# A convolution bias moved from the matmul engine to ScalarE, and segment sums with one stationary matrix and split rates moving

## The chip, the cores and the metric

One core of a Trainium2 chip runs the whole program. The time is the device time of that core in microseconds, from launch to end. Besides TensorE (PE), the engines are VectorE (DVE), ScalarE (ACT), GpSimd (POOL) and SyncE (SP), which issues most of the DMAs.

## The reference, cut to what matters

The program is one layer of a hybrid decoder for a prompt of 2048 tokens and 8 sample tokens. The change touches the Mamba-2 (SSD) mixer of the prompt. Its two pieces are a depthwise causal convolution with a bias, followed by silu, and a scan in chunks of 128 tokens, in which a lower triangle of sums of the rates `a` between two tokens is exponentiated:

```python
def causal_dwconv(xpad, w, bias):          # w: 4 taps, 896 channels
    y = bias
    for j in range(K):
        y = y + xpad[:, j:j + T] * w[j]
    return y

xbc_c = jax.nn.silu(causal_dwconv(xpad, conv_w, conv_b))
...
xr = jnp.where(jnp.tril(jnp.ones((T, T), bool), -1), a[..., :, None], 0.0)
ss = jnp.cumsum(xr, axis=-2)               # segsum: ss[l, s] = a[s+1] + ... + a[l]
scores = einsum(Cc, Bc) * jnp.exp(ss)      # per head, 6 heads, 16 chunks
```

All is in float32.

## The kernel before, in words

The program runs its stages one after the other: the input projection, forgetting attention (with the sample's paged cache beside it), `local_stage`, an output projection, and the channel mixer. Only `local_stage` is touched. It works on two things side by side. The first is dilated attention in 48 units of 128 queries (three dilation groups of 16 units). The second is the SSD mixer in 16 chunks of 128 tokens. A slot `s` holds one step of several units; a chunk takes three slots, called phase 0, 1 and 2 (`s % 3`). Each engine has its program written out slot by slot, in a fixed order, with semaphores between engines; no engine goes ahead of its own order.

What each engine does for a chunk `c`, in its order:

- PE, phase 0: the unit's `value`, `turn_p`, `score`, then `turn_x` of the chunk before (L1507; it waits for the activated x part and for `y_taken`, which DVE gives with L1411), `turn_in` (L1481, seven transposes of the raw input into the PSUM banks `conv_ps`), the unit's `turn` (L1446), and `segments` (L1530, six matmuls, one for each head, into two PSUM banks). Phase 1: `turn_b`, and `convolve(c, 0)` for one channel tile. Phase 2: `states`, `convolve(c, 1)` for three channel tiles, `outputs` (L1555). A channel tile is five matmuls: one with the bias on a diagonal against ones (L1496) and four with the taps on diagonals against shifted input (L1498).
- POOL: `xdd` (L1131) in phase 0, `mix` (L1140), `skip` (L1145) and the convolution of one x tile (L1112 to L1116) in phase 1, then in phase 2 `mask` of the next chunk (L1099): it multiplies a 128x128 step matrix by the rates of six heads, 768 elements a partition, into `a_mask`. These six products are the stationary sides of `segments`.
- ACT: among the units' copies and exponentials, `tanh` of the x part (L1255) and of the other four tiles straight from PSUM (L1259) in phase 2, `decay` = exp of the segment sums (L1240) in phase 0.
- DVE: the units' `copy_p` (L1308) and `maxima` (L1322 to L1328), the convolution of two x tiles (L1336, L1341) in phase 1, and in phase 2 the state (L1395, L1398), `y` from PSUM (L1400), then `activate(c, 0)` and `activate(c, 1)` (both L1355: (tanh + 1) times the convolved value; half 0 reads SBUF alone, half 1 reads its second operand from PSUM), then L1411 (y plus PSUM, gives `y_taken`), L1415, L1419.

The taps and the bias were halved beforehand, since silu is computed as x/2 (1 + tanh(x/2)). Before the loop the stage builds the diagonals (DVE L1281, ACT L1161), the gates and the distance biases of the attention.

Of the kernel before, what the change touches and what calls it, by code (L numbers as in the profile page):

```python
# [12 lines left out]
F32 = mybir.dt.float32  # L13
# [908 lines left out]
def local_stage(nc, inputs, pa, pb, toep_d, gates, ma, mc, p_ssm_d, p_conv_d, ahead_of_projection):  # L922
# [9 lines left out]
    with ExitStack() as ctx:  # L932
# [3 lines left out]
        def sem(name):  # L936
# [16 lines left out]

        a = sb("sp_a", [P, ALL_TILES, H])
        dt = sb("sp_dt", [P, ALL_TILES, H])
        e_cum = sb("sp_e_cum", [P, ALL_TILES, H])
# [3 lines left out]
        xT = sb("sp_xT", [P, 2, CT, C_CONV - 1 + P])  # L960
        diag = sb("sp_diag", [P, CT, C_CONV + 1, P])
        x_conv = sb("sp_x_conv", [P, XT, P])
        x_part = sb("sp_x_part", [P, P])
        tanh = sb("sp_tanh", [P, CT, P])
        sT = sb("sp_sT", [P, 2, CT, P])
        z2 = sb("sp_z2", [P, 2, C_INNER])
# [5 lines left out]
        b_tok = sb("sp_b_tok", [P, C_GROUPS, C_STATE])  # L972
        a_mask = sb("sp_a_mask", [P, H, P])
        decay = sb("sp_decay", [P, 2, H, P])
# [34 lines left out]
             "cb_ready", "mix_ready", "st_done", "off_ready", "y_done", "y_taken", "y_ready", "state_ready", "skip_ready",  # L1009
             "squared"))  # L1010
        fin_turned, fin_ready, out_done = sem("sp_fin_turned"), sem("sp_fin_ready"), sem("sp_out_done")
        dve, gps = Steps(sem("sp_dve")), Steps(sem("sp_gps"))
# [82 lines left out]
        def _(pool):  # L1095
            def mask(c):
                if c >= 1:
                    pool.wait_ge(seg_done, c)
                pool.tensor_tensor(a_mask[:], consts[:, TRI_GT].unsqueeze(1).to_broadcast([P, H, P]),  # L1099
                                   a[:, c + 1].unsqueeze(2).to_broadcast([P, H, P]), ALU.mult).then_inc(mask_ready, 1)  # L1100

# [19 lines left out]
            pool.wait_ge(inputs.landed, inputs.LANDED)  # L1121
            pool.wait_ge(gates_a, 1)
            mask(0)
# [31 lines left out]
        def _(act):  # L1155
# [3 lines left out]
            for k in range(5, CT):  # L1159
                for j in range(C_CONV + 1):  # L1160
                    last = act.activation(diag[:, k, j], ident, ACT.Copy, scale=taps[:, k, j:j + 1])  # L1161
            last.then_inc(diag_late, 1)
# [39 lines left out]
            for s in range(SLOTS):  # L1202
# [47 lines left out]
                if phase == 2 and now < TILES:  # L1250
                    act.wait_ge(x_conv_ready, now + 1)
                    act.wait_ge(x_conv_low, now + 1)
                    if now >= 1:
                        act.wait_ge(s_ready, 2 * now - 1)
                    act.activation(tanh[:, 0:XT], x_conv[:], ACT.Tanh).then_inc(tanh_ready, 1)  # L1255
                    act.wait_ge(conv_done, 2 * now + 2)
                    if now >= 1:
                        act.wait_ge(s_ready, 2 * now)
                    act.activation(tanh[:, XT:].rearrange("p c n -> p (c n)"), conv_ps[:, XT * P:CT * P], ACT.Tanh  # L1259
                                   ).then_inc(tanh_ready, 1)  # L1260

        @block.vector
        def _(v):
# [6 lines left out]
            v.tensor_tensor(a[:], dt[:], heads[:, 0].unsqueeze(1).to_broadcast([P, ALL_TILES, H]), ALU.mult  # L1270
                            ).then_inc(gates_a, 1)
            dve.link(v, v.tensor_scalar(taps[:], taps[:], 0.5, None, ALU.mult))
            v.sem_inc(taps_ready, 1)
# [5 lines left out]
            def diagonals(c, taps_of):  # L1279
                for j in taps_of:  # L1280
                    last = v.tensor_scalar(diag[:, c, j], ident, taps[:, c, j:j + 1], None, ALU.mult)  # L1281
                last.then_inc(diag_ready, 1)
# [14 lines left out]
            by_distance(4)  # L1297
            diagonals(XT, range(3, C_CONV + 1))
            by_distance(5)
            diagonals(XT + 1, range(C_CONV + 1))  # L1300
            v.wait_ge(gates_exp, 3)

# [46 lines left out]
            def activate(c, half):  # L1349
                lo, hi = (XT, CT) if half else (0, XT)  # L1350
                v.wait_ge(tanh_ready, 2 * c + half + 1)
                if c >= 2:
                    v.wait_ge(st_done, c - 1)
                pre = conv_ps[:, XT * P:CT * P].rearrange("p (c n) -> p c n", n=P) if half else x_conv[:]
                v.scalar_tensor_tensor(out=sT[:, c % 2, lo:hi], in0=tanh[:, lo:hi], scalar=1.0, in1=pre,  # L1355
                                       op0=ALU.add, op1=ALU.mult).then_inc(s_ready, 1)
# [69 lines left out]
        def _(pe):  # L1426
# [49 lines left out]
            def turn_in(c):  # L1476
                pe.wait_ge(landed[c % 2], 16 * (c // 2 + 1))
                if c >= 1:
                    pe.wait_ge(s_ready, 2 * c)
                for k in range(CT):  # L1480
# [4 lines left out]
            def convolve(c, half):  # L1485
# [8 lines left out]
                for k in range(*((4, CT) if half else (XT, 4))):  # L1494
                    at = conv_ps[:, k * P:(k + 1) * P]
                    pe.matmul(at, diag[:, k, C_CONV], consts[:, ONES], start=True, stop=False)  # L1496
                    for j in range(C_CONV):
                        last = pe.matmul(at, diag[:, k, j], xT[:, c % 2, k, j:j + P], start=False,  # L1498
                                         stop=(j == C_CONV - 1))
# [22 lines left out]
            def segments(c):  # L1522
# [4 lines left out]
                if c == 1:  # L1527
                    pe.wait_ge(decay_ready, 1)
                for h in range(H):
                    last = pe.matmul(seg_ps[:, h // HG, (h % HG) * P:(h % HG + 1) * P], a_mask[:, h], tri,  # L1530
                                     start=True, stop=True)
                last.then_inc(seg_done, 1)
# [2032 lines left out]
```

## Time and profile before

| | |
|---|---|
| median of 3 runs | 3129.94 us (3129.54 to 3137.76) |
| the profiled execution, first to last instruction | 3133.8 us |
| PE busy | 2985.0 us, 95% |
| DVE, ACT, POOL busy | 51%, 28%, 24% |
| mean granted clock of TensorE | 0.975 of 2.4 GHz |
| `local_stage` | from about 1047 to about 1345 us |

No own time of the profiled execution stands in the page beside its span of 3133.8 us, which lies between the lowest and the highest of the three runs. The share of PE is a mean over stages; only the 300 us of `local_stage` bear on this change, so the rows below are from there, with a few from other stages for prices. Times in rows are microseconds from the start of the span. In a timeline row the first number is the start, the second the time from that start to the end of the group, and brackets give the idle time before it and what ended that. A float32 matmul with two full operands leaves two records on PE (512 of L1498 for the program's 256), a transpose leaves one.

### The profile page before, as it was taken

To read this page: it belongs to the slowest core of one execution; us is meant where nothing else is said; L and a number is where in the kernel's file an instruction comes from. 1 tells how busy PE (TensorE), PEld (TensorE's weight loads), DVE (VectorE), ACT (ScalarE), POOL (GpSimd) and SP (SyncE) were. 2 spreads that over 40 slices of the span, in tenths; PEclk is the share of its full clock that TensorE was granted. 3 is DMA by queue.
4 is the path that set the end of the run, shared out by engine and by line. 5 is a ranking of instruction groups with operands and counts; after the bars stand their busy time and mean duration, and the time that the engine had idled before them with its cause. 6 is when DMAs were issued, how large, how long until landed. Compare 5 with 4: busy or idle time off the path is not lost. (4 is left out here: it accounts for less than half of the span.)

```text
span 3133.8 us, 45320 instructions
## 1 busy us (share of the span) xinstructions
PE 2985.0 (95%) x16457; PEld 2560.7 (82%) x16457; DVE 1613.1 (51%) x2998; ACT 870.3 (28%) x1670; POOL 746.9 (24%) x512
## 2 busy tenths in 40 slices
PE   8999999989999899979979999999999999999997
PEld 5888889867676799867769999999997788888886
DVE  5113210267687588856645555445556544444445
ACT  4223321233332456533332111122214111111112
POOL 4002100134443254522202221111222211122210
PEclk9999999999999899989989999999999999999999
DMA  4455335567674343358651111111113311111101
GB/s 150 166 202 182 116 133 159 144 193 200 200 213 128 105 124 104 80 145 242 207 216 62 41 40 40 55 66 41 41 54 121 136 52 40 41 50 58 54 14 55
DMA packets 237384, 350.26 MB, mean 112 GB/s; under 512 B 75337, under 2 KB 172138, under 8 KB 231263
## 3 DMA queue, kind: packets, MB, share of 16 engines
q1 hardware_dynamic: 236295, 325.80, 33.6%
q0 software_dynamic: 944, 22.61, 1.9%
q8 instruction: 81, 1.33, 0.2%
q14 instruction: 64, 0.52, 0.1%
HBM read 283.53 MB, written 93.97 MB: 120 GB/s over the span
## 5 line engine op out<-in xcount | busy, mean ns | idle before, releaser
L2639 POOL TENSOR_TENSOR cm_dn_lo<-cm_dn_raw,cm_dn_hi 128x1024 fp32r<-128x1024 f32 x44 | 108.3, 2483 | 974.0 <-ACT cm_dn_hi L2688 974.0
L3376 PE MATMUL pj_acc<-pj_w_hi,pj_h_hi 128*128 128x480 f32 (+3 forms) x896 | 335.2, 374 | 0.9 <-DVE pj_h_lo L3251 0.9
L3377 PE MATMUL pj_acc<-pj_w_lo,pj_h_hi 128*128 128x480 f32 (+3 forms) x896 | 333.4, 372 | 0.0
L3378 PE MATMUL pj_acc<-pj_w_hi,pj_h_lo 128*128 128x480 f32 (+3 forms) x896 | 333.1, 372 | 0.0
L2932 PE MATMUL cm_g_ps<-cm_h_hi,cm_up_hi 128*128 128x344 f32 (+1 forms) x880 | 310.1, 352 | 11.6 <-DVE cm_h_lo L2744 11.2
L2934 PE MATMUL cm_g_ps<-cm_h_hi,cm_up_lo 128*128 128x344 f32 (+1 forms) x880 | 308.5, 351 | 0.0
L2932 PE MATMUL cm_u_ps<-cm_h_hi,cm_up_hi 128*128 128x344 f32 (+1 forms) x880 | 308.2, 350 | 0.0
L2934 PE MATMUL cm_u_ps<-cm_h_hi,cm_up_lo 128*128 128x344 f32 (+1 forms) x880 | 307.8, 350 | 0.0
L2933 PE MATMUL cm_g_ps<-cm_h_lo,cm_up_hi 128*128 128x344 f32 (+1 forms) x880 | 307.7, 350 | 0.0
L2933 PE MATMUL cm_u_ps<-cm_h_lo,cm_up_hi 128*128 128x344 f32 (+1 forms) x880 | 307.0, 349 | 0.0
L3257 DVE TENSOR_TENSOR pj_w_lo<-area,pj_w_hi 128x480 fp32r<-128x480 f32 (+3 forms) x112 | 75.6, 697 | 381.5 <-ACT pj_w_hi L3213 381.4
L2632 POOL TENSOR_TENSOR cm_up_lo<-area,cm_up_hi 128x2048 fp32r<-128x2048 f32 x42 | 195.5, 4656 | 176.6 <-ACT cm_up_hi L2664 176.6
L2767 DVE TENSOR_SCALAR area<-area 128x344 f32<-128x344 f32 (+2 forms) x110 | 54.2, 493 | 330.9 <-ACT area L2681 190.6
L2677 ACT ACTIVATE area<-cm_g_ps 128x344 f32<-128x344 f32 (+1 forms) x110 | 55.1, 511 | 510.0 <-PE cm_g_ps L2934 509.9
L2932 PEld LDWEIGHTS cm_g_ps<-cm_h_hi,cm_up_hi 128*128 128x128 f32 x880 | 165.9, 188 | 36.8 <-issue 21.7
L3376 PEld LDWEIGHTS pj_acc<-pj_w_hi,pj_h_hi 128*128 128x128 f32 x896 | 169.9, 190 | 23.3 <-issue 3.9
L3377 PEld LDWEIGHTS pj_acc<-pj_w_lo,pj_h_hi 128*128 128x128 f32 x896 | 169.8, 189 | 17.7
L3378 PEld LDWEIGHTS pj_acc<-pj_w_hi,pj_h_lo 128*128 128x128 f32 x896 | 169.8, 189 | 17.7
L2933 PEld LDWEIGHTS cm_g_ps<-cm_h_lo,cm_up_hi 128*128 128x128 f32 x880 | 166.0, 189 | 15.9
L2934 PEld LDWEIGHTS cm_g_ps<-cm_h_hi,cm_up_lo 128*128 128x128 f32 x880 | 166.0, 189 | 15.8
L2934 PEld LDWEIGHTS cm_u_ps<-cm_h_hi,cm_up_lo 128*128 128x128 f32 x880 | 165.4, 188 | 16.0
L2933 PEld LDWEIGHTS cm_u_ps<-cm_h_lo,cm_up_hi 128*128 128x128 f32 x880 | 165.3, 188 | 15.9
(448 smaller groups left out, 6472.0 us busy)
## 6 DMA issues: line engine op xcount, KB each, us to landing
area<-in_w_up SPq DMA_DIRECT2D x44, 1024.0 KB, 7.2
fp_kv_low<-in_fox_kv SPq DMA_DIRECT2D x168, 256.0 KB, 3.0
area<-in_fox_kv SPq DMA_DIRECT2D x88, 256.0 KB, 3.0
cm_dn_raw<-in_w_down SPq DMA_DIRECT2D x44, 512.0 KB
out_s_win<-in_cache POOLq DMA_DIRECT2D x8, 2047.0 KB, 9.0
proj_a<-area SPq DMA_DIRECT2D x48, 240.0 KB
sp_raw<-proj_b SPq DMA_DIRECT2D x16, 640.0 KB, 4.0
area<-in_w_a SPq DMA_DIRECT2D x10, 960.0 KB, 7.2
```

What stands on the lines that cost most here:

```text
L2632: pool.tensor_tensor(up_lo[:, s], up_raw[:, s], up_hi[:, s].bitcast(F32), ALU.subtract).then_inc(up_ready, 1)
L2639: pool.tensor_tensor(dn_lo[:, s], dn_raw[:, s], dn_hi[:, s].bitcast(F32), ALU.subtract).then_inc(dn_ready, 1)
L2677: act.activation(gate[:, s, HALO + at[b]:HALO + at[b + 1]], g_ps[:, b, 0:H.widths[b]], ACT.Copy).then_inc(gate_ready, 1)
L2767: dve.link(v, v.tensor_scalar(conv[:, 0:ws], gate[:, s, at[b]:at[b] + ws], taps[0], tap_b, ALU.mult, ALU.add))
L2932: pe.matmul(out, hi, h_hi[:, k, cs], start=(k == 0), stop=False)
L2933: pe.matmul(out, hi, h_lo[:, k, cs], start=False, stop=False)
L2934: last = pe.matmul(out, lo, h_hi[:, k, cs], start=False, stop=(k == KT - 1))
L3257: v.tensor_tensor(w_lo[:, j % 2, k, 0:n], w_raw[:, k, 0:n], w_hi[:, j % 2, k, 0:n].bitcast(F32), ALU.subtract).then_inc(w_ready, 1)
L3376: pe.matmul(out, h_hi[:, k, place(t)], w_hi[:, j % 2, k, 0:wide], start=(k == 0), stop=False)
L3377: pe.matmul(out, h_hi[:, k, place(t)], w_lo[:, j % 2, k, 0:wide], start=False, stop=False)
L3378: last = pe.matmul(out, h_lo[:, k, place(t)], w_hi[:, j % 2, k, 0:wide], start=False, stop=(k == KT - 1))
```

## The change

The bias: `diag` loses its bias diagonal, `convolve` starts with the first tap (four matmuls a tile instead of five), and ACT copies each of the four tiles out of PSUM with ACT.Identity and the bias as a per-partition operand into a new SBUF tile `pre`. It then waits for its own four copies and takes the tanh of `pre` in SBUF. `activate(c, 1)` on DVE reads `pre` instead of PSUM, and `turn_in` waits for `pre_ready` instead of `s_ready`.

The segment sums: the stationary side becomes one float32r matrix `after` for all heads. What moves is `a_steps`, the upper step matrix times the rates, where the rates are split into a float32r part and its remainder. POOL's `mask` so writes 2 x 6 x 128 = 1536 elements a partition instead of 768, and `segments` becomes four float32r matmuls of 128x384 (two groups of three heads, two parts summed in PSUM) instead of six float32 ones of 128x128. Three DVE instructions before the loop make `after` and the parts.

```diff
-        diag = sb("sp_diag", [P, CT, C_CONV + 1, P])
+        diag = sb("sp_diag", [P, CT - XT, C_CONV, P])
+        pre = sb("sp_pre", [P, CT - XT, P])
-        a_mask = sb("sp_a_mask", [P, H, P])
+        a_steps = sb("sp_a_steps", [P, 2, H, P], F32R)
@@ mask, on POOL
-                pool.tensor_tensor(a_mask[:], consts[:, TRI_GT].unsqueeze(1).to_broadcast([P, H, P]),
-                                   a[:, c + 1].unsqueeze(2).to_broadcast([P, H, P]), ALU.mult).then_inc(mask_ready, 1)
+                pool.tensor_tensor(a_steps[:].rearrange("p k h n -> p (k h) n"),
+                                   tri.unsqueeze(1).to_broadcast([P, 2 * H, P]),
+                                   a_parts[:, c + 1].rearrange("p k h -> p (k h)").bitcast(F32).unsqueeze(2)
+                                   .to_broadcast([P, 2 * H, P]), ALU.mult).then_inc(mask_ready, 1)
@@ ACT, before the loop and in phase 2
-                for j in range(C_CONV + 1):
-                    last = act.activation(diag[:, k, j], ident, ACT.Copy, scale=taps[:, k, j:j + 1])
+                for j in range(C_CONV):
+                    last = act.activation(diag[:, k - XT, j], ident, ACT.Copy, scale=taps[:, k, j:j + 1])
-                    act.activation(tanh[:, XT:].rearrange("p c n -> p (c n)"), conv_ps[:, XT * P:CT * P], ACT.Tanh
-                                   ).then_inc(tanh_ready, 1)
+                    for k in range(XT, CT):
+                        last = act.activation(pre[:, k - XT], conv_ps[:, k * P:(k + 1) * P], ACT.Identity,
+                                              bias=taps[:, k, C_CONV:C_CONV + 1])
+                    last.then_inc(pre_ready, 1)
+                    act.wait_ge(pre_ready, now + 1)
+                    act.activation(tanh[:, XT:], pre[:], ACT.Tanh).then_inc(tanh_ready, 1)
@@ DVE
+            v.wait_ge(gates_a, 1)
+            v.tensor_copy(after[:], consts[:, TRI_GT])
+            dve.link(v, v.tensor_copy(a_parts[:, :, 0], a[:]))
+            v.tensor_tensor(a_parts[:, :, 1], a[:], a_parts[:, :, 0].bitcast(F32), ALU.subtract).then_inc(steps_ready, 1)
-                pre = conv_ps[:, XT * P:CT * P].rearrange("p (c n) -> p c n", n=P) if half else x_conv[:]
-                v.scalar_tensor_tensor(out=sT[:, c % 2, lo:hi], in0=tanh[:, lo:hi], scalar=1.0, in1=pre,
+                v.scalar_tensor_tensor(out=sT[:, c % 2, lo:hi], in0=tanh[:, lo:hi], scalar=1.0, in1=pre[:] if half else x_conv[:],
@@ PE
-                    pe.wait_ge(s_ready, 2 * c)
+                    pe.wait_ge(pre_ready, c)
-                    pe.matmul(at, diag[:, k, C_CONV], consts[:, ONES], start=True, stop=False)
                     for j in range(C_CONV):
-                        last = pe.matmul(at, diag[:, k, j], xT[:, c % 2, k, j:j + P], start=False,
+                        last = pe.matmul(at, diag[:, k - XT, j], xT[:, c % 2, k, j:j + P], start=(j == 0),
-                for h in range(H):
-                    last = pe.matmul(seg_ps[:, h // HG, (h % HG) * P:(h % HG + 1) * P], a_mask[:, h], tri,
-                                     start=True, stop=True)
+                for g in range(C_GROUPS):
+                    for k in range(2):
+                        last = pe.matmul(seg_ps[:, g], after[:],
+                                         a_steps[:, k, g * HG:(g + 1) * HG].rearrange("p h n -> p (h n)"),
+                                         start=(k == 0), stop=(k == 1))
```

## Rows read from the trace of the kernel before

**Rows 1.** The page: the span, and part 1, busy time of the engines.
```profile
span 3133.8 us, 45320 instructions
PE 2985.0 (95%) x16457; PEld 2560.7 (82%) x16457; DVE 1613.1 (51%) x2998; ACT 870.3 (28%) x1670; POOL 746.9 (24%) x512
```
**Rows 2.** Busy time by stretch, inside the stage; the first row names the columns.
```profile
core 0: us, PE busy (x) PEld busy (x) DVE busy (x) ACT busy (x) POOL busy (x), PEclk, DMA share, GB/s
1110.00:1160.00 50.00, 49.27 (x429) 48.66 (x429) 44.56 (x124) 27.54 (x93) 26.97 (x38) 1.00 0.46 128
...
1260.00:1310.00 50.00, 45.53 (x384) 43.78 (x383) 43.64 (x135) 30.03 (x107) 27.96 (x40) 1.00 0.38 96
```
**Rows 3.** Timeline of PE: one convolution tile, the segments, and float32r matmuls elsewhere.
```profile
1168.17 0.39 PE L1496 MATMUL sp_m_ps<-sp_consts,sp_diag 128*128 128x128 f32 x2
...
1169.29 0.39 PE L1496 MATMUL sp_m_ps<-sp_consts,sp_diag 128*128 128x128 f32 x2
...
1176.18 1.50 PE L1530 MATMUL sp_m_ps<-sp_consts,sp_a_mask 128*128 128x128 f32 x12
...
2000.02 0.32 PE L2932 MATMUL cm_u_ps<-cm_h_hi,cm_up_hi 128*128 128x344 f32 x1
2000.18 0.32 PE L2933 MATMUL cm_u_ps<-cm_h_lo,cm_up_hi 128*128 128x344 f32 x1
```
**Rows 4.** Timeline of DVE: one chunk of the first group, from one copy_p to the next.
```profile
1089.88 0.69 DVE L1308 COPY dp_pT<-dp_w 128x512 f32<-128x512 f32 x1 [2.03 <-PE dp_w L1463]
...
1099.40 0.55 DVE L1395 TENSOR_TENSOR sp_state<-sp_state,sp_e_all 128x384 f32<-128x384 f32 x1
...
1100.92 0.77 DVE L1355 SCALAR_TENSOR_TENSOR sp_sT<-sp_tanh,sp_x_conv 128x384 f32<-128x384 f32 x1
1101.61 0.67 DVE L1355 SCALAR_TENSOR_TENSOR sp_sT<-sp_tanh,sp_m_ps 128x512 f32<-128x512 f32 x1
1102.21 0.54 DVE L1411 TENSOR_TENSOR sp_y<-sp_y,sp_m_ps 128x384 f32<-128x384 f32 x1
...
1108.02 0.69 DVE L1308 COPY dp_pT<-dp_w 128x512 f32<-128x512 f32 x1 [2.06 <-PE dp_w L1463]
```
**Rows 5.** Timelines of POOL, ACT and PE in the same chunk.
```profile
1099.42 1.85 POOL L1099 TENSOR_TENSOR sp_a_mask<-sp_consts,sp_a 128x768 f32<-128x768 f32 x1
...
1100.18 0.51 ACT L1255 ACTIVATE sp_tanh<-sp_x_conv 128x384 f32<-128x384 f32 x1
1100.60 0.57 ACT L1259 ACTIVATE sp_tanh<-sp_m_ps 128x512 f32<-128x512 f32 x1
...
1103.31 0.49 PE L1507 MATMUL sp_m_ps<-sp_consts,sp_sT 128*128 128x128 f32 x3
...
1107.33 0.66 PE L1463 MATMUL dp_w<-sp_consts,dp_probs 128*128 128x128 f32 x4 [0.37 <-ACT dp_probs L1180]
```
**Rows 6.** Timeline of a chunk of the third group, and L1355 of the last chunk.
```profile
1276.21 1.47 POOL L1099 TENSOR_TENSOR sp_a_mask<-sp_consts,sp_a 128x768 f32<-128x768 f32 x1
...
1276.90 1.18 DVE L1355 SCALAR_TENSOR_TENSOR sp_sT<-sp_tanh,sp_x_conv 128x384 f32<-128x384 f32 x1
...
1278.61 0.54 DVE L1411 TENSOR_TENSOR sp_y<-sp_y,sp_m_ps 128x384 f32<-128x384 f32 x1
...
1279.29 0.52 PE L1507 MATMUL sp_m_ps<-sp_consts,sp_sT 128*128 128x128 f32 x3 [0.82 <-DVE sp_y L1411]
...
1326.14 0.55 DVE L1355 SCALAR_TENSOR_TENSOR sp_sT<-sp_tanh,sp_x_conv 128x384 f32<-128x384 f32 x1
```
**Rows 7.** Prices of other sizes: POOL products from timeline and page, ACT copies from timelines.
```profile
1106.05 0.83 POOL L1131 TENSOR_TENSOR sp_xdd<-sp_xd,sp_e_rest 128x384 f32<-128x384 f32 x1 [4.77 <-DVE sp_xd L1371]
...
L2632 POOL TENSOR_TENSOR cm_up_lo<-area,cm_up_hi 128x2048 fp32r<-128x2048 f32 x42 | 195.5, 4656 | 176.6 <-ACT cm_up_hi L2664 176.6
...
1049.01 3.03 ACT L1161 ACTIVATE sp_diag<-sp_consts,sp_taps 128x128 f32<-128x128 f32 x10 [1.23 <-DVEq L1273]
...
1160.44 0.28 ACT L1193 ACTIVATE dp_kT<-dp_w 128x128 f32<-128x128 f32 x1
```

More of the change, by code:

```diff
@@ L954, in local_stage @@
         a = sb("sp_a", [P, ALL_TILES, H])
+        a_parts = sb("sp_a_parts", [P, ALL_TILES, 2, H], F32R)
+        after = sb("sp_after", [P, P], F32R)
         dt = sb("sp_dt", [P, ALL_TILES, H])
@@ L1010, in local_stage @@
              "squared"))
+        pre_ready, steps_ready = sem("sp_pre_ready"), sem("sp_steps_ready")
         fin_turned, fin_ready, out_done = sem("sp_fin_turned"), sem("sp_fin_ready"), sem("sp_out_done")
@@ L1121, in _ @@
             pool.wait_ge(inputs.landed, inputs.LANDED)
-            pool.wait_ge(gates_a, 1)
+            pool.wait_ge(steps_ready, 1)
             mask(0)
@@ L1280, in diagonals @@
                 for j in taps_of:
-                    last = v.tensor_scalar(diag[:, c, j], ident, taps[:, c, j:j + 1], None, ALU.mult)
+                    last = v.tensor_scalar(diag[:, c - XT, j], ident, taps[:, c, j:j + 1], None, ALU.mult)
                 last.then_inc(diag_ready, 1)
@@ L1297, in _ @@
             by_distance(4)
-            diagonals(XT, range(3, C_CONV + 1))
+            diagonals(XT, range(3, C_CONV))
             by_distance(5)
-            diagonals(XT + 1, range(C_CONV + 1))
+            diagonals(XT + 1, range(C_CONV))
             v.wait_ge(gates_exp, 3)
```

## The prediction

> **What bounds the kernel now.** The page first: PE is busy 95% of a span of 3133.8 us [rows 1]. That is a mean over five stages, and it would suggest that every matmul taken away is gained. The busy time by stretch narrows it to the stage of the change. There PE is at 99% early and at 91% late, DVE at 89% and 87%, ACT near 60%, POOL near 55%, at full clock [rows 2]. Two engines are near their limit, so shares don't decide. The timeline does, read as a cycle of one chunk.
>
> Take the wait of DVE for PE at L1308, which comes once a chunk. From 1089.88 to 1108.02 a chunk takes 18.14 us [rows 4]. It has two halves. In the first, DVE runs almost without a gap from L1308 to the end of L1411 at 1102.75 (1102.21 + 0.54), 12.87 us. Then PE starts L1507, which waits for L1411, at 1103.31, and from there it is 4.71 us (transposes, ACT's copies, the exponentials, L1463) to the next L1308. In this second half PE itself waits 0.37 us for ACT ahead of L1463 [rows 5], so a PE that is faster there brings nothing. PE's own work matters only before L1507, and how much can be read off as the gap between L1411's end and L1507's start. In this chunk it is 0.56 us, with no idle time of PE before it: PE comes last. In the chunk of the third group it is 0.14 us (1278.61 + 0.54 = 1279.15, L1507 at 1279.29), and PE sat idle 0.82 us [rows 6]: DVE comes last. Of the chunk turns in the timeline six look like the first (starts 1085 to 1158 and 1228) and eight like the second (1175, 1193, 1210, 1245, 1263, 1279, 1296, 1312), besides the first turn at 1067 and the last at 1328. The least gap being 0.15, PE can be the later one by 0.41 us at most.
>
> **The part that looks like the gain: PE.** A convolution tile of five matmuls takes 1.12 us from start to start (1168.17 to 1169.29), so one takes 0.224 us; four tiles lose one each, 0.90 us a chunk. Segments are six such matmuls, 12 records, 1.34 us. A float32r matmul of 344 columns follows the one before by 0.16 us (2000.02 to 2000.18) [rows 3]; for 384 columns I take 0.175, so four take 0.70 us and 0.64 is saved. PE thus loses 1.54 us of work a chunk, 25 us in 16 chunks. But the segments lie in the half where PE waits for ACT: they bring nothing. The 0.90 us lie before L1507 and bring at most 0.41 us in six chunks, 2.5 us in all. Bounds for that saving: 0 and 2.5; I take 2.5.
>
> **The part that costs: POOL's mask, through DVE.** The row to look at is the first L1355. It takes 1.18 us at 1276.90 and 0.55 us at 1326.14 in the last chunk, which has no mask [rows 6]. The mask of that earlier chunk ends at 1276.21 + 1.47 = 1277.68, and L1355 ends at 1278.08, 0.40 later. In the early chunk the mask ends at 1101.27 and L1355 at 1101.69, 0.42 later [rows 4, 5]. It is so in every chunk with a mask: this DVE instruction, both inputs of which lie in SBUF, gets under way only when POOL's is over. L1398, L1400 and the second L1355, with an input in PSUM, keep their 0.55 and 0.67. The other way round, the mask that starts together with L1395 (1099.42 and 1099.40) shows 1.85 instead of 1.47: it is POOL that waits there. So the mask's end, not ACT and not the conversion, times the first L1355, and everything behind it on DVE: the second L1355, L1411, and with it PE's L1507.
>
> The Trainium skill says the same of the mechanism ("SBUF — State Buffer", Who interferes with whom): a DVE instruction with two inputs in SBUF and a GpSimd instruction that reads SBUF exclude each other, and the second to come blocks for the whole of the first. By that rule the second L1355, which now reads `pre` from SBUF, could block too; it doesn't change the sum, because it comes behind the first, when the mask is over.
>
> How long is the new mask? Its work doubles from 768 to 1536 elements. Prices of POOL: 384 elements with one operand repeated along the row take 0.83 us [rows 7], 768 take 1.47 [rows 6], hence 0.64 us for 384 more, 1.67 ns an element. Then 1536 take 1.47 + 1.28 = 2.75 us: 1.28 more. The upper bound is the float32r output with two full inputs, 2048 elements in 4.656 us [rows 7], 2.27 ns an element, 3.49 us: 2.0 more. The lower bound is no growth, 0. I take 1.28, as the operands keep their shape and the row nearest to it is the mask itself.
>
> The anchor of the mask doesn't move: POOL reaches it through the mix, skip and convolution work that starts from DVE's L1378, so POOL and DVE keep their distance. The first L1355 stalls 1.28 us longer. Behind it on DVE nothing has slack until L1411, behind that PE waits, and the 4.71 us follow unchanged. In eight chunk turns this is + 1.28 us: 10.2. In the six where PE was later by 0.41: + 0.87 each: 5.2.
>
> **The edges.** In the first chunk there is the same mask, over the last of L1341 and the first tanh, with slack only later: + 1.1. In the last chunk no mask runs; there ACT's new work is bare (next paragraph): + 1.2. Before the loop DVE gets three small instructions (an estimate of 0.75 us, at the 0.25 us that instructions of such a size take there), ahead of a wait of 0.98 us for PE which hides them; ACT builds 8 diagonals instead of 10 of 0.30 us [rows 7]: 0. Sum: 10.2 + 5.2 + 1.1 + 1.2 = 17.7 us.
>
> **ACT's edit, costed at nothing, and its cover.** Four copies of 128x128 with a bias: a plain one takes 0.28 and a scaled one 0.30 from start to start [rows 7], so 1.2 us at most (0.7 if they overlap), then a wait for itself, about 0.1, and the tanh from SBUF about 0.05 longer. The second tanh then ends about 1.3 us later: in the third group from 1277.29 to 1278.6. DVE wants it after the first L1355, by the new mask at 1279.3; 0.7 us of cover. In the early chunk the tanh ends at 1101.17 + 1.3 = 1102.5, the first L1355 at 1102.97. So the cover is the mask itself. Without it (a mask that doesn't hold DVE longer) ACT would make the second L1355 later by about 0.6 in the third group and 0.9 less 0.41 in the first. Behind ACT's new wait are queued the unit's copy out L1172 and the copy for L1507; L1172 moves by 1.3 us, and PE's `turn` asks for it over 1 us after L1507 starts: covered. `turn_in`'s new wait lies behind L1507 and is met by then: nothing.
>
> **How the span stands to the median.** 3133.8 is 3.9 us above the median of 3129.94, inside the spread of the three runs. The stage is followed by a stage that starts when it ends, so the sum passes to the end in full: 3129.94 + 17.7, about 3147.6 us.
>
> **The rivals.**
> 1. *ACT's chain in the mask's place.* The mask hardly holds DVE (POOL works at a better rate, or the rate matrix broadcast twice is cheap). Then 8 x 0.6 + 6 x 0.5 + 1.2 is 9 us at the high end, 3 us with overlapped copies: 3133 to 3139. For it: the ACT chain is real and near; against it: the mask's row grew steadily from 384 to 768 elements. Chance 0.12.
> 2. *PE is the bound after all* (the faster side). Its point: PE's 0.90 us ahead of L1507 and 0.64 us after it pass to the time if what follows DVE's L1411 isn't what PE waits for. For it: 99% busy in [rows 2]. Against it: the idle time of PE ahead of L1507 and L1463. It needs DVE's run to get shorter by as much, for which the change has nothing. It would give up to 25 us: 3105, or 3115 if the segments alone are covered. Chance 0.07.
> 3. *A dearer mask.* 2.0 us instead of 1.28: 14 x 0.72 = 10 us more, 3158. For it: all float32r outputs of POOL in the page are at that rate; against it: they have two full inputs. Chance 0.12.
> 4. *Segments don't get cheap* (the float32r matmul takes as long per column as float32: 4 x 3 x 0.224 = 2.7 us, 1.35 more, of which PE's wait of 0.37 covers a part: 0.9 x 16 = 14 us on top): 3162. Against it are the rows of 344 columns. Chance 0.02.
>
> **How the numbers follow.** The forecast has 0.67: 3143 to 3152 for its own roundings (1.0 to 1.6 us a mask). With rivals 1 and 3 the range is 3135 to 3159. Within 0.3% means within 9.4 us, about what a measurement can tell: rival 1 is there, and a small part of the forecast. Faster 0.07, same 0.14, slower 0.79.
>
> **What the profile after would show.** L1099 with 1536 elements at about 2.75 us; the first L1355 still ending 0.4 us behind the mask, at about 2.4 us instead of 1.18; idle time of PE ahead of L1507 in all chunks, 1.5 to 2 us; chunk turns of about 19.0 and 17.7 us instead of 18.14 and 16.44; second tanh ended before the second L1355 could start. PE busy about 25 us less in all, DVE busy more. I am wrong if the mask takes less than 2 us, if the first L1355 isn't tied to its end, or if L1507 starts earlier after L1308 than now.

## The result and the profile after

The changed kernel takes 3156.28 us (median of 5, 3149.95 to 3164.73), the kernel before, run beside it, 3134.01 (median of 5, 3129.54 to 3137.76). The ratio is 1.0083, with a 95% interval of 1.0060 to 1.0106: about 26 us slower, where 17.7 were forecast. The two medians alone differ by 22.3 us. The new median lies above the 3143 to 3152 of the forecast itself, and inside the wide range up to 3159.

The profiled execution took 3149.95 us, with a span of 3148.2, and its stages outside the one that was changed took 12.7 us less than in the profile of before. The two spans (3133.8 and 3148.2) therefore differ by 14.4 us only, and the stage itself by more. From here on "the stage" runs from DVE's first bias instruction to the first DVE instruction of the stage that follows: 1047.61 to 1348.27, 300.66 us, before; 1038.28 to 1366.01, 327.73 us, after. That is 27.1 us more, which agrees with the ratio.

The page of the kernel after: the span, and part 1, busy time of the engines (before is in [rows 1]).
```profile
span 3148.2 us, 44871 instructions
...
PE 2964.4 (94%) x16201; PEld 2544.8 (81%) x16201; DVE 1632.7 (52%) x2999; ACT 886.2 (28%) x1732; POOL 767.1 (24%) x512
```
PE is busy 20.6 us less, DVE 19.6 and POOL 20.2 more. PE's number isn't the 25 us of the forecast come true. Only 6.7 us of it lie in the stage (277.31 before, 270.61 after), and 12.9 lie ahead of it, where nothing was changed and the mean granted clock was 0.96 in the one execution and 0.98 in the other. What the change saves is read from one chunk of the first group at full clock, first before, then after:
```profile
1102.21:1120.35 18.14, 17.77 (x157) 17.52 (x156) 15.56 (x45) 10.41 (x36) 9.27 (x13) 1.00 0.43 121
1096.99:1116.04 19.05, 16.47 (x138) 16.01 (x138) 16.85 (x45) 11.46 (x39) 10.55 (x13) 1.00 0.41 115
```
That is 1.30 us of PE's time a chunk, 21 us in 16, where 1.54 were forecast. In the stage's sum most of it is hidden, because matmuls at half the clock are busy for longer.

Busy time by stretch of the kernel after, to set beside [rows 2].
```profile
core 0: us, PE busy (x) PEld busy (x) DVE busy (x) ACT busy (x) POOL busy (x), PEclk, DMA share, GB/s
1110.00:1160.00 50.00, 42.42 (x359) 41.21 (x358) 43.77 (x115) 30.58 (x105) 26.80 (x32) 1.00 0.37 103
1160.00:1210.00 50.00, 43.93 (x358) 42.85 (x356) 44.75 (x119) 29.70 (x104) 30.65 (x38) 0.97 0.46 131
1210.00:1260.00 50.00, 42.55 (x329) 41.43 (x330) 41.73 (x116) 29.83 (x104) 24.11 (x31) 0.93 0.30 80
1260.00:1310.00 50.00, 40.55 (x291) 39.27 (x290) 43.13 (x119) 26.76 (x94) 28.27 (x37) 0.87 0.34 88
```
PE's share fell from 99 to 85% early and from 91 to 81% late. The column after POOL is the one to look at: the granted clock, 1.00 in all four stretches before, falls here to 0.87 by the last. The forecast has no term for it.

Timelines of POOL, ACT, DVE and PE in a chunk of the first group, after (before: [rows 4, 5]).
```profile
1092.92 3.13 POOL L1103 TENSOR_TENSOR sp_a_steps<-sp_consts,sp_a_parts 128x1536 fp32r<-128x1536 f32 x1
...
1094.09 1.12 ACT L1266 ACTIVATE sp_pre<-sp_m_ps,sp_taps 128x128 f32<-128x128 f32 x4
1095.23 0.63 ACT L1270 ACTIVATE sp_tanh<-sp_pre 128x512 f32<-128x512 f32 x1
...
1094.41 2.05 DVE L1368 SCALAR_TENSOR_TENSOR sp_sT<-sp_tanh,sp_x_conv 128x384 f32<-128x384 f32 x1
1096.39 0.68 DVE L1368 SCALAR_TENSOR_TENSOR sp_sT<-sp_tanh,sp_pre 128x512 f32<-128x512 f32 x1
1096.99 0.54 DVE L1424 TENSOR_TENSOR sp_y<-sp_y,sp_m_ps 128x384 f32<-128x384 f32 x1
...
1097.68 0.52 PE L1519 MATMUL sp_m_ps<-sp_consts,sp_sT 128*128 128x128 f32 x3 [1.40 <-DVE sp_y L1424]
```
Line by line this is the forecast: the mask is 1.28 us longer than 1.85; the first activation product ends at 1096.46, 0.41 after the mask's end at 1096.05, and takes 2.05 us instead of 0.77; the second follows at once and keeps its 0.68, since the mask is over; the second tanh ended at 1095.86, before anyone wanted it; PE's transposes (L1519, before L1507) wait 1.40 us for DVE. The turn of this chunk is 19.05 us, 0.91 more than 18.14 (0.87 forecast).

The same in the third group, where the gap is (before: [rows 6]).
```profile
1283.74 2.74 POOL L1103 TENSOR_TENSOR sp_a_steps<-sp_consts,sp_a_parts 128x1536 fp32r<-128x1536 f32 x1
...
1284.43 2.47 DVE L1368 SCALAR_TENSOR_TENSOR sp_sT<-sp_tanh,sp_x_conv 128x384 f32<-128x384 f32 x1
...
1288.11 0.88 PE L1519 MATMUL sp_m_ps<-sp_consts,sp_sT 128*128 128x128 f32 x3 [2.78 <-DVE sp_y L1424]
1288.78 1.70 PE L1494 MATMUL sp_m_ps<-sp_consts,sp_raw 128*128 128x128 f32 x7
```
The mask and the product are at the forecast sizes again. But PE had been idle 2.78 us, and the transposes then take 0.88 us instead of 0.52. The windows around them say why.
```profile
1284.00:1286.00 2.00, 1.33 (x12) 1.14 (x11) 2.00 (x3) 1.97 (x7) 2.00 (x1) 1.00 0.62 223
1286.00:1288.00 2.00, 0.00 (x0) 0.00 (x0) 1.97 (x3) 0.18 (x2) 0.48 (x1) 0.76 0.00 0
1288.00:1290.00 2.00, 1.89 (x9) 1.92 (x10) 1.93 (x9) 0.49 (x1) 0.00 (x0) 0.50 0.03 8
1290.00:1292.00 2.00, 2.00 (x10) 2.00 (x9) 0.65 (x3) 1.46 (x5) 0.83 (x1) 0.50 0.00 0
1292.00:1294.00 2.00, 1.90 (x10) 1.71 (x9) 0.24 (x1) 2.00 (x8) 0.00 (x0) 0.53 0.00 0
1294.00:1296.00 2.00, 2.00 (x21) 2.00 (x19) 1.81 (x12) 1.56 (x8) 0.43 (x1) 1.00 0.41 102
```
With PE at rest (busy 0.00 from 1286 to 1288) the granted clock falls from 1.00 to 0.50, from 2.4 to 1.2 GHz, and it stays there for some 7 us of nearly full work. This is just the half of the cycle in which everything waits for PE.

Where the 27.1 us of the stage lie, in three pieces cut at DVE's L1424 (L1411 before). The forecast's 17.7 us are sorted the same way. The 14 turns run from 1084.10 to 1327.21 before and from 1077.93 to 1343.47 after.

| piece | forecast | measured |
|---|---|---|
| from the stage's start to the first L1424 (36.49 us before, 39.65 after) | 1.1 + 1.28 = 2.4 | 3.2 |
| 5 turns of the first group (90.06, 94.64) | 5 x 0.87 = 4.4 | 4.6 |
| 5 turns of the middle (88.01, 96.36) | 5 x 1.28 - 0.41 = 6.0 | 8.4 |
| 4 turns of the third group (65.04, 74.54) | 3 x 1.28 + 1.2 = 5.0 | 9.5 |
| from the last L1424 to the end (21.06, 22.54) | 0 | 1.5 |

The first group is right to 0.2 us. What is missing lies, but for the two ends, in the turns whose granted clock is under 1.00: 0.91 in three of the middle five, 0.83 to 0.90 in the last four.

### The profile page after: what moved, and what is told of

Read it like the earlier page. It is cut to its first block and busy times, and to the rows that moved or that the text cites. A ratio compares the mean times of both kernels' runs of the same rounds, so it can differ in the third digit from the quotient of the medians.

```text
span 3148.2 us, 44871 instructions
## 1 busy us (share of the span) xinstructions
PE 2964.4 (94%) x16201; PEld 2544.8 (81%) x16201; DVE 1632.7 (52%) x2999; ACT 886.2 (28%) x1732; POOL 767.1 (24%) x512
## 5 line engine op out<-in xcount | busy, mean ns | idle before, releaser
L2948 PEld LDWEIGHTS cm_g_ps<-cm_h_hi,cm_up_lo 128*128 128x128 f32 x880 | 166.1, 189 | 15.7
```

The source lines that it names most:

```text
L2948: last = pe.matmul(out, lo, h_hi[:, k, cs], start=False, stop=(k == KT - 1))
```

## The experiments

All are timed against the kernel before on the same chip, whose median is 3128 to 3131 us there. "Early" is a turn of the first group (18.14 us before), "late" one of the third (16.44 before). A stage's time comes from one profiled execution of each kernel, so a microsecond or two between two stages says little: the changed kernel gave 327.73 and 329.43. The turns repeat to a few hundredths wherever the clock is at 1.00.

### Each half of the change alone

**Bias alone.** The kernel before with the bias part of the change: this edit of ACT's, and four matmuls a tile instead of five.
```diff
-                    act.activation(tanh[:, XT:].rearrange("p c n -> p (c n)"), conv_ps[:, XT * P:CT * P], ACT.Tanh
-                                   ).then_inc(tanh_ready, 1)
+                    for k in range(XT, CT):
+                        last = act.activation(pre[:, k - XT], conv_ps[:, k * P:(k + 1) * P], ACT.Identity,
+                                              bias=taps[:, k, C_CONV:C_CONV + 1])
+                    last.then_inc(pre_ready, 1)
+                    act.wait_ge(pre_ready, now + 1)
+                    act.activation(tanh[:, XT:], pre[:], ACT.Tanh).then_inc(tanh_ready, 1)
```


> Only the bias is moved to ACT; mask and segments are as before. Theory (DVE's run sets the cycle, POOL's mask times its first L1355): the mask still ends after 1.47 us, so the new ACT work is bare. From the start of the first tanh to the end of the second it takes 2.2 us in the changed kernel, against 1.0 before: the second L1355 starts about 0.8 us later in the first group, less the 0.41 by which PE was the later one, and 0.5 later in the third. 6 x 0.4 + 8 x 0.5 + 1.2 + 1.2 = 9 us slower than before (7 to 13 with some dips of the clock), stage 308 to 314 us instead of 300.7. Rival (PE is the bound): 0.90 us of matmuls less a chunk, 14 us faster, stage 286.

Measured: ratio 1.0035 (1.0013 to 1.0057), stage 310.71 us, 10 more than before. Early turns take 18.57 us, late ones 16.95 at full clock; two late turns had a clock of 0.90 and 0.91 and took about 1 us more. The line that carries it, DVE in a late chunk:
```profile
1298.44 0.69 DVE L1360 SCALAR_TENSOR_TENSOR sp_sT<-sp_tanh,sp_pre 128x512 f32<-128x512 f32 x1 [0.44 <-ACT sp_tanh L1266]
```
With the old mask ACT's chain is bare, by 0.44 us here and 0.71 early. So the cover of the forecast was indeed the mask, and rival 2 (PE is the bound) falls: 0.90 us of PE's work less in every chunk, and the stage got longer.

**Segments alone.** Before, with the split rates, the float32r mask and its four matmuls.
```diff
-        a_mask = sb("sp_a_mask", [P, H, P])
+        a_steps = sb("sp_a_steps", [P, 2, H, P], F32R)
...
-                for h in range(H):
-                    last = pe.matmul(seg_ps[:, h // HG, (h % HG) * P:(h % HG + 1) * P], a_mask[:, h], tri,
-                                     start=True, stop=True)
+                for g in range(C_GROUPS):
+                    for k in range(2):
+                        last = pe.matmul(seg_ps[:, g], after[:],
+                                         a_steps[:, k, g * HG:(g + 1) * HG].rearrange("p h n -> p (h n)"),
+                                         start=(k == 0), stop=(k == 1))
```


> Only the segment sums are changed (mask of 1536 elements, four float32r matmuls); the bias stays on PE. Theory: the first L1355 stalls 1.28 us longer, PE has no relief ahead of L1507, so + 0.87 in six chunk turns and + 1.28 in eight, + 1.1 in the first: 17 us slower than before, stage 318 (up to 322 if the clock dips in places). Rival (the ACT chain is what costs in the changed kernel): no change, 0 to 3 us. Rival (PE is the bound): 0.64 us a chunk faster, 10 us.

Measured: ratio 1.0061 (1.0040 to 1.0082), stage 319.73, 19 more. Early turns 19.05, late 17.72 at full clock; three turns had a clock of 0.90 or 0.91. The matmuls are cheap (the group of four takes 0.94 us where twelve records took 1.50), so rival 4 falls, but they bring nothing.

**The mask's length alone.** Before, with a mask twice as long whose second half nobody reads; PE and ACT have exactly the work of before.
```diff
-        a_mask = sb("sp_a_mask", [P, H, P])
+        a_mask2 = sb("sp_a_mask", [P, 2, H, P])
+        a_mask = a_mask2[:, 0]
...
-                pool.tensor_tensor(a_mask[:], consts[:, TRI_GT].unsqueeze(1).to_broadcast([P, H, P]),
-                                   a[:, c + 1].unsqueeze(2).to_broadcast([P, H, P]), ALU.mult).then_inc(mask_ready, 1)
+                pool.tensor_tensor(a_mask2[:].rearrange("p k h n -> p (k h) n"),
+                                   consts[:, TRI_GT].unsqueeze(1).to_broadcast([P, 2 * H, P]),
+                                   a2[:, c + 1].rearrange("p k h -> p (k h)").unsqueeze(2)
+                                   .to_broadcast([P, 2 * H, P]), ALU.mult).then_inc(mask_ready, 1)
```


> The kernel before, with POOL's mask doubled to 1536 elements (the second half is not used); PE, ACT and DVE do what they did in the loop. Before the loop DVE makes two copies of the rates. Theory: this alone brings + 0.87 in six chunk turns, + 1.28 in eight, + 1.1 in the first: 17 us slower, stage 318, the first L1355 at 2.05 to 2.47 us instead of 0.77 to 1.18. With PE's old work in place few dips of the clock. Rival (a longer mask is free, since POOL idles 9 us a chunk): no change.

Measured: ratio 1.0087 (1.0054 to 1.0120), stage 320.56, 20 more. POOL and DVE in an early chunk:
```profile
1101.67 3.13 POOL L1102 TENSOR_TENSOR sp_a_mask<-sp_consts,sp_a 128x1536 f32<-128x1536 f32 x1
...
1103.16 2.05 DVE L1363 SCALAR_TENSOR_TENSOR sp_sT<-sp_tanh,sp_x_conv 128x384 f32<-128x384 f32 x1
```
The same 3.13 and 2.05 as in the changed kernel, turns of 19.06 and 17.75. One POOL instruction that is twice as long, off every dependency of DVE, costs the kernel all that the segments' part costs (19.9 against 19.1 us of stage). That settles what the mask does. Some 2 of these 20 us are the clock: here too three late turns had 0.90 or 0.91. In the changed kernel, where PE has still less to do ahead of L1519 (idle time 1.40 us early instead of 0.72), it is seven.

The Trainium skill says of this ("SBUF — State Buffer", Who interferes with whom) that DVE with two inputs in SBUF and a GpSimd instruction reading SBUF exclude each other for a whole instruction. The trace agrees: 0.55 us without a mask in [rows 6], 2.05 and 2.47 here, always ended 0.4 us after the mask.

### What the clock costs

**The outputs' matmuls twice.** The changed kernel, with the six matmuls of the outputs issued a second time into the same place: 1.34 us more of PE's work in a chunk, in the half where PE has slack.
```diff
-                for h in range(H):
+                for h in [*range(H), *range(H)]:
                     last = pe.matmul(y_ps[:, h * HD:(h + 1) * HD], mix[:, h], xd[:, h], start=True, stop=True)
```


> The changed kernel with the six matmuls of `outputs` issued twice (same operands, same place, the second overwrites the first), ahead of y_done: 1.34 us more of PE work a chunk, in the stretch where PE now idles 1.4 to 2.9 us ahead of L1519. Theory: the part of the loss that the forecast lacked, about 9 us, is the granted clock, which falls to 0.5 behind the long idle times in later chunks; with PE busy there it stays at 1.0, and the added work is free: 6 to 10 us faster than the changed kernel, stage 318 to 321, clock above 0.97 between 1110 and 1310. Rival (the clock falls for another reason, PE's work counts): stage 328 to 349, 0 to 21 us slower than the changed kernel.

Measured: ratio 1.0061 (1.0043 to 1.0080), stage 324.20 where 318 to 321 were expected. By stretch, early and late:
```profile
1110.00:1160.00 50.00, 47.31 (x401) 46.25 (x402) 44.57 (x119) 30.03 (x104) 29.44 (x38) 1.00 0.46 131
...
1260.00:1310.00 50.00, 42.94 (x356) 41.42 (x356) 44.03 (x120) 30.80 (x110) 30.94 (x39) 1.00 0.39 100
```
The clock is at 1.00 in all 14 turns. Idle time of PE ahead of L1519 is 0 early and 1.43 us late, instead of 1.40 and 2.8. The turns of the three groups are + 4.6, + 6.1 and + 5.0 us over before: 15.7, against 15.4 forecast. In the changed kernel they are + 22.4. So the 6.7 us between are the granted clock's, and more matmuls made these turns faster. The stage gained only 3.5 of them, because its first piece took 43.49 us instead of 39.65. That piece was 42.71 in the next run, which has no added matmuls, so most of the difference isn't their doing. In whole runs the gain doesn't stand clear of the noise: 1.0061 and the 1.0083 of the changed kernel have intervals that overlap. What is shown is the clock and the length of the turns.

**The changed kernel again**, on the chip of the last runs.

> The changed kernel once more, beside e12. If the dips of the clock go with the long idle times of PE ahead of L1519 (2 us and more in the third group), they stand again in the late chunks and not in the first five: stage 325 to 330, chunk turns of 19.05 us in the first group at full clock. If they are an accident of that one execution, they are elsewhere or gone.

Measured: ratio 1.0078 (1.0064 to 1.0093), stage 329.43. Early turns 19.05 again, late ones 18.8 to 19.0 at clocks of 0.82 to 0.91. Falls of the clock belong to the kernel, not to one execution. Which turns they hit varies: one of the middle five here, three in the first execution.

### Moving the mask away

The obvious remedy is to let POOL build the mask elsewhere. In all that follow it is issued right behind `xdd`, in the first phase of the chunk instead of the third.
```diff
-                c = chunk(s, -1, 2)
-                if c is not None:
-                    mask(c)
...
                                        ).then_inc(xdd_ready, 1)
+                c = chunk(s, -1, 0)
+                if c is not None:
+                    mask(c)
```
**In the changed kernel.**

> The changed kernel with POOL's mask of 1536 elements moved from phase 2 to phase 0, behind xdd, where POOL idles 3 to 4 us and DVE works on PSUM sources. Nothing else differs. Theory: the first L1355 is back at 0.55 us in all chunks and the ACT chain sets the second one: 7 to 12 us slower than before, stage 308 to 312 instead of 327.7. The mask itself still takes 2.75 us. Rival (the mask's length is not the cause; float32r matmuls or ACT are): stage stays at 325 or more.

Measured: ratio 1.0069 (1.0044 to 1.0094), stage 319.14, where 308 to 312 were expected. The first product is back at 0.55 us and the second waits 0.93 to 1.12 us for ACT: both as expected. Early turns are 18.66, but late ones 17.68 instead of 16.9 even at full clock, and three of the last four turns had a clock of 0.82 to 0.90. Something else was late.

**In the kernel before**, and **with the segments' part only**.

> The kernel before with its mask moved to phase 0, behind xdd. Theory: the first L1355 at 0.55 us; that is 0.22 us earlier in the first group, where PE was the later one (no gain), and 0.63 earlier in the third, where PE idled 0.5 to 0.8 us (gain): 2 to 4 us faster, stage 297 to 299. Rival (order on POOL doesn't matter): 0.

> The segment sums changed and the mask moved, the bias left on PE. Theory: the long mask is then free, and the cheaper segments lie where PE waits for ACT: as e5, 2 to 4 us faster than before, stage 297 to 299. Rival (PE is the bound once DVE is free): 0.64 us a chunk more, stage 287.

Measured: stages 297.34 (ratio 1.0006, 0.9977 to 1.0035), as expected, and 299.95 (1.0001, 0.9979 to 1.0022), 1 us more than expected. Both have early turns of 18.14, where PE is the later one; late turns are 15.80 and 16.50. By the ratios neither differs from the kernel before; the gain of the first is seen in its turns alone. Here the missing 0.7 us shows. POOL and DVE in the third group, first with the short mask, then with the long one:
```profile
1260.19 1.47 POOL L1099 TENSOR_TENSOR sp_a_mask<-sp_consts,sp_a 128x768 f32<-128x768 f32 x1
...
1262.10 0.17 DVE L1327 TENSOR_SCALAR dp_neg<-dp_top 128x2 f32<-128x2 f32 x1
```
```profile
1260.48 2.75 POOL L1102 TENSOR_TENSOR sp_a_steps<-sp_consts,sp_a_parts 128x1536 fp32r<-128x1536 f32 x1
...
1262.38 0.88 DVE L1336 TENSOR_SCALAR dp_neg<-dp_top 128x2 f32<-128x2 f32 x1
1263.24 0.41 DVE L1387 TENSOR_TENSOR sp_cb<-sp_m_ps,sp_consts 128x256 f32<-128x256 f32 x1
```
An instruction on two elements takes 0.88 us instead of 0.17, and ends at 1263.26 where the mask ends at 1263.23. The short mask is over before it (1261.66). It has one input in SBUF, not two. The same row stands in the moved changed kernel (0.88 at 1270.10) and explains 0.7 of the 0.8 us that its late turns were too long. The Trainium skill has this case too (same section): `tensor_scalar` can enter a mode that uses both ports, and then it contends with GpSimd; the trace agrees, by these 0.7 us.

With the segments' part, the stage is 0.7 us shorter than before's 300.66; with the old segments 3.3 shorter. The cheap matmuls bring nothing even where their mask is as harmless as it gets.

**Mask moved and outputs twice.**

> The changed kernel with the mask moved (e4, stage 319.1, which was forecast at 308 to 312 and showed a clock of 0.82 to 0.90 in three late chunks) and the matmuls of `outputs` issued twice, 1.34 us more PE work a chunk where PE idled 0.9 to 2.7 us. Theory: what e4 lost against its forecast is the clock; with PE kept busy the clock stays at 1.0 to the last chunk and the stage takes 308 to 313, the late chunk turns 16.9 instead of 18.2 to 18.6. Rival (e4's loss has another cause): 319 or more.

Measured: ratio 1.0061 (1.0047 to 1.0076), stage 318.36; 308 to 313 were expected. The clock is 1.00 in all four stretches, and the late turns are 17.67, as they were in the kernel without the added matmuls wherever its clock held. So the clock isn't what keeps the moved kernel long: it is worth 0.3 to 0.9 us in single turns there, 1.7 us in the third group (71.63 and 69.93), and the added matmuls cost 0.7 of that again in the first (93.09 and 93.82). The held `dp_neg` and ACT's bare chain are the rest, and the late turns price them one by one: 15.80 with the short mask moved, 16.50 with the long one (0.7 for `dp_neg`), 17.67 with the bias on ACT as well (1.17, where the second half waits 1.07 for ACT).

### Moving ACT's chain out of the way

**Second half of the activation later in the same phase**, behind L1424.
```diff
                     activate(c, 0)
-                    activate(c, 1)
...
                                     ).then_inc(y_taken, 1)
+                c = chunk(s, 0, 2)
+                if c is not None:
+                    activate(c, 1)
```


> The changed kernel with the mask moved and, on DVE, the second L1368 (which the ACT chain feeds) placed behind L1424 instead of ahead of it; the changed kernel allows it, since turn_in waits for pre_ready and no longer for s_ready. Theory: ACT's new work and 0.6 us of DVE leave the way to L1519; PE's relief of 0.90 us counts in the first group, 1.2 us in the third: 6 x 0.9 + 8 x 1.2 = 15 us faster than before (11 to 18), stage 283 to 289. Rival (the later second half delays DVE's maxima and with them ACT's exponentials by 0.6 us a chunk): 5 us faster or less.

Measured: ratio 1.0017 (0.9997 to 1.0037), stage 307.88, where 283 to 289 were expected. The second half still waits 0.47 to 0.66 us for ACT at its new place, and now the maxima stand behind it, hence the exponentials, hence PE in its critical half. From the transposes to L1480, which needs the exponentials, it takes 4.64 us:
```profile
1100.11 0.49 PE L1523 MATMUL sp_m_ps<-sp_consts,sp_sT 128*128 128x128 f32 x3
...
1104.75 0.66 PE L1480 MATMUL dp_w<-sp_consts,dp_probs 128*128 128x128 f32 x4 [0.92 <-ACT dp_probs L1186]
```
In the changed kernel it takes 4.05 (1097.68 to this row):
```profile
1101.73 0.66 PE L1476 MATMUL dp_w<-sp_consts,dp_probs 128*128 128x128 f32 x4 [1.01 <-ACT dp_probs L1186]
```
So the half is 0.6 us longer. The wait in brackets doesn't show this by itself. It was 0.37 in [rows 5] and is 1.01 in the changed kernel only because PE is done with the cheaper segments 0.64 us earlier. In the late turns `dp_neg` is held as well (1.74 us instead of 0.17), and four turns, early ones among them, have a clock of about 0.90.

**A phase later**, ahead of `xd`: the tanh is long done by then.
```diff
                 c = chunk(s, 1, 0)
                 if c is not None:
+                    activate(c, 1)
                     v.wait_ge(x_ready, c + 1)
```


> The changed kernel with the mask moved to phase 0 on POOL, and the second half of the activation on DVE moved out of phase 2 altogether, into the next phase 0 ahead of xd, where DVE idles about 2 us. In e7 it sat between L1424 and the maxima and there waited for ACT (0.5 to 0.7 us) and delayed the exponentials. Theory: now nothing of ACT's new work lies in the cycle; the first group goes by PE's way from L1322 to L1519, 0.9 us shorter than before, so 17.24 us a chunk instead of 18.14, the third group by DVE's, 15.2 instead of 16.44: 15 us faster than before, stage 284 to 290 if the clock holds, some 5 us more if it dips. Rival (DVE's second half collides with POOL's xdd and mask, or turn_b waits for it): no gain over e5, stage 297 or more.

Measured: ratio 0.9996 (0.9984 to 1.0008), stage 299.89, where 284 to 290 were expected. Early turns 17.63, half a microsecond under before. Late turns 16.51: the long mask now runs over `dp_neg` for 1.3 to 1.6 us (1.77 us at 1260.60, 1.47 at 1277.41).

**The same with the old segments and the short mask.**

> As e9, but with the segment sums of the kernel before (mask of 768 elements, six float32 matmuls): the bias alone on ACT, mask moved, second half in phase 0. Theory: the segments lie where PE waits for ACT, so their 0.64 us are free here and even keep PE busier: stage as e9 or 1 to 4 us shorter where e9 shows dips of the clock. Rival (PE is the bound of the stage now): 0.64 us a chunk longer than e9, 10 us.

Measured: ratio 0.9981 (0.9966 to 0.9996), 3122.81 us against 3130.55, stage 290.48, 9.4 less than the one above where 0 to 4 were expected. Early turns 17.47, late 15.24. DVE and the windows:
```profile
1262.92 0.55 DVE L1360 SCALAR_TENSOR_TENSOR sp_sT<-sp_tanh,sp_x_conv 128x384 f32<-128x384 f32 x1
...
1266.07 0.68 DVE L1360 SCALAR_TENSOR_TENSOR sp_sT<-sp_tanh,sp_pre 128x512 f32<-128x512 f32 x1
...
1110.00:1160.00 50.00, 48.54 (x421) 47.69 (x420) 43.86 (x128) 33.55 (x115) 25.05 (x37) 1.00 0.45 126
...
1260.00:1310.00 50.00, 45.90 (x386) 43.97 (x384) 45.35 (x146) 35.34 (x127) 27.85 (x42) 1.00 0.34 81
```
PE is at 97 and 92%, and the clock stays up. This is the one version whose interval lies below 1, if barely, by 0.2%: it keeps the bias part of the change, moves the mask and the second half, and leaves the segments' part out.

## Why the prediction was right and wrong

**Right: the sign, and what the time hangs on.** Sorted by what the runs isolate:
- POOL's mask through DVE. Forecast 2.75 us; measured 2.74. First product forecast at about 2.4; measured 2.47 late. The doubled mask alone gave + 19.9 us of stage.
- The 0.41 us by which PE could be the later one early: turns of 19.05 against 19.0, and of 17.72 against 17.7 where a late turn kept its clock, which the changed kernel's own never did (segments alone, outputs twice).
- PE's saving worth nothing behind L1411: yes. The 0.64 us of the segments turned into a longer wait for ACT, 1.01 us instead of 0.37. The saving itself was 21 us rather than 25; no term of the sum hung on that.
- ACT at nothing under the mask: yes. With the short mask 0.4 us early (0.9 less 0.41 forecast) and 0.5 late (0.6).
- The rivals: 1 would have needed a mask that doesn't hold DVE; 2 and 4 fall by the first two runs; 3 by the mask's 2.74 us. The measured time lay near rival 3's 3158, but not for its reason.

**Wrong: the size.** The step that failed is the sentence "behind that PE waits, and the 4.71 us follow unchanged". It took the second half of the cycle as a constant. The forecast itself listed "idle time of PE ahead of L1507 in all chunks, 1.5 to 2 us" as a sign to look for, and didn't ask what this idle time does to PE. It was 1.4 us early, where the clock stayed at 1.00, and 1.8 to 2.9 us in eight later turns. In seven of these the granted clock fell to 1.2 GHz about when PE's critical half began, for 3.4 us in five turns and 6.8 in two (0.83 to 0.91 over the whole turn), and the turn grew by 0.4 to 1.5 us over its forecast. In the second execution it was five turns of seven with 2.0 to 2.8 us, and none with less. Before, with idle times of 0.82 at most, no turn fell. In the terms of the sum:
- 14 turns: 15.4 forecast, 22.4 measured, 15.7 with the clock held up. The difference of 6.7 is the clock.
- After the last L1424: 0 forecast, 1.5 measured. From L1519 to the start of the outputs' matmuls it is 11.49 us (1344.16 to 1355.65), where before it was 9.95 (1327.90 to 1337.85). In that stretch four matmuls of 192 columns take 1.49 us; before they took 0.82. So this is the clock too: 0.69 over the piece, 0.83 before (low for 10.2 us instead of 3.4).
- The first piece: 2.4 forecast, 3.2 measured. PE's first transposes waited 3.17 us and then took 0.91:
```profile
1058.87 0.91 PE L1519 MATMUL sp_m_ps<-sp_consts,sp_sT 128*128 128x128 f32 x3 [3.17 <-DVE sp_sT L1368]
```
 The clock was low for 3.4 us from about there. In the two kernels with the long mask and the bias on PE it didn't fall in this place, and the piece took 38.92 and 38.95 us, 2.4 and 2.5 more than before, as forecast. In the second execution of the changed kernel it was low for 6.8 us and the piece took 42.71; with the outputs twice 10.2 us, and 43.49. So the 0.8 us go with the clock as well. The bias alone, with no fall here, made the piece 0.5 us longer, and no run separates the two.

The missing 6.7, 1.5 and 0.8 us, and 0.3 us between 15.7 and 15.4, make 9.3 of the 9.4 us between 27.1 and 17.7.

**Beliefs of the experiments that fell.** That the long mask would be free in the first phase: it holds a two-element `tensor_scalar` by 0.7 us, and by up to 1.6 once the turns get shorter. That the activation's second half could wait on DVE's queue behind L1424: what it delays there is the exponentials.

**Still open.** Which idle times let the clock fall. One turn with 1.99 us kept it, and with the bias alone it fell after 1.68 us and held after 2.02, twice. In the kernel with the second half behind L1424 it fell after waits of only 0.43 and 0.92 us close together, while the changed kernel's early turns have 1.40 and 1.01 and kept it. No run here varied the idle time in small steps.

## What to carry to other kernels

When an off-path instruction on POOL gets longer, look at which DVE instructions that read SBUF alone run beside it, small ones too: the ones seen here ended with it or 0.4 us behind, and a dependency graph doesn't show it. When a forecast leaves PE idle for longer than it is now, read the second half of the cycle again at 1.2 GHz before calling it unchanged; taking work off a PE that isn't the bound can let its clock fall, and useless matmuls in its slack can hold it up. An activation whose input has just become later is best consumed a phase later, not a few instructions later.

## What the runs showed of the hardware

- One POOL product of 1536 elements, one operand repeated along the row: 2.74 us, 1.28 more than for 768. Begun together with DVE's L1408, with two inputs in SBUF, it takes 3.13. DVE's first activation product, with both inputs in SBUF, takes 0.55 us alone and ended 0.40 to 0.43 us behind POOL's end whenever it came under it, in each of the 14 chunks of the kernel before and of the changed one.
- A `tensor_scalar` on 128x2 elements in SBUF takes 0.17 us alone and 0.88, 1.47 and 1.77 us under a POOL product.
- In the 14 turns of the changed kernel, after 1.8 to 2.9 us of idle time of PE in one piece, the granted clock went to 0.50 in 7 turns of 8, and in a second execution, after 2.0 to 2.8 us, in 5 of 7; after 1.4 to 1.5 us in none, nor once after 1.83. It was low for 3.4 us in eight of these twelve and for 6.8 in four. Three transposes: 0.52 us at full clock, 0.88 to 0.91 at half; seven: 0.93 and 1.70; four float32r matmuls of 384 columns: 0.94 and 1.63.
- Four 128x128 `Identity` activations with a bias, out of PSUM: 1.12 us, 0.28 each, and 0.63 for a tanh of 512 columns out of SBUF (0.57 out of PSUM before).
